# Scratch matrices of a chunked recurrence in DRAM: laid out by rows of all slots, diagonal blocks moved in four transfers

## The reference

```python
def rwkv7_scan(r, w, k, v, kk, a, reverse):      # 16 heads of 64, f32
    def step(state, inp):
        r_t, w_t, k_t, v_t, kk_t, a_t = inp
        sa = jnp.einsum('bhvk,bhk->bhv', state, kk_t)
        state = (state * w_t[:, :, None, :]
                 - sa[..., None] * (kk_t * a_t)[:, :, None, :]
                 + v_t[..., None] * k_t[:, :, None, :])
        return state, jnp.einsum('bhvk,bhk->bhv', state, r_t)
```

## Time and profile before

| | us |
|---|---|
| median of 3 runs (lowest to highest) | 1600.93 (1599.67 to 1605.68) |
| the profiled execution, own time | 1600.83 |
| its span | 1599.0 |
| TensorE busy | 1461.1 (91%) |
| VectorE busy | 510.5 (32%) |
| ScalarE busy | 240.1 (15%) |
| GpSimd busy | 184.5 (12%) |

### The profile page before, as it was taken

The page is one execution under the profiler, slowest core; times in us unless marked ns, Lnnn a source line. Parts: engine busy times, 40 slices in busy tenths (PEclk is TensorE's granted clock), DMA queues, the critical chain, the costliest instruction groups (busy, mean ns, idle before and its releaser), DMA issues.

```text
span 1599.0 us, 26196 instructions
## 1 busy us (share of the span) xinstructions
PE 1461.1 (91%) x11376; PEld 735.6 (46%) x11376; DVE 510.5 (32%) x712; ACT 240.1 (15%) x478; POOL 184.5 (12%) x349
## 2 busy tenths in 40 slices
PE   7999999989888895899989989989989989989987
PEld 5344455878877653434324324324324324324322
DVE  6666534667664564101101101101101101101103
ACT  3333321222212121100000000000000000000002
POOL 1323504434333210000000000000000000000000
PEclk9999999999998997899999999999999999999999
DMA  9245577766765645499999999999999999999994
GB/s 302 66 158 185 183 264 161 176 136 133 149 111 127 263 172 210 187 428 425 421 428 422 425 427 426 425 425 427 423 426 426 425 424 428 423 425 427 422 425 184
DMA packets 186070, 500.47 MB, mean 313 GB/s; under 512 B 125904, under 2 KB 135248, under 8 KB 153216
## 3 DMA queue, kind: packets, MB, share of 16 engines
q1 hardware_dynamic: 180192, 479.31, 78.2%
q0 software_dynamic: 5792, 19.88, 3.6%
HBM read 470.83 MB, written 28.33 MB: 312 GB/s over the span
## 4 chain that ended last, share of the span: by engine, by line
PE 32%; DMA 23%; DVE 2%; issue 1%; ACT 1%; DVEq 0%; SPq 0%
DMA ring<-in_exp_w_up 23%; PE pD L1543 14%; PE pG L1504 6%; PE pU L1524 6%; PE pX L1492 4%; PE pG L1524 3%; DVE res L1652 1%; DVE hid L1670 1%; PE pX L1531 1%; ACT hidT L1613 0%; DVE res L1688 0%; ACT xin L1596 0%; PE pX L1560 0%; ACT xin L1628 0%; ACT L1631 0%
## 5 line engine op out<-in xcount | busy, mean ns | idle before, releaser
L1670 DVE TENSOR_TENSOR hid<-silu,pU 128x512 f32<-128x512 f32 x32 | 20.6, 684 | 774.5 <-PE pU L1524 774.5
L1524 PE MATMUL pU<-ring,xin 128*64 128x512 f32 x768 | 173.8, 597 | 37.8 <-DMA ring<-in_exp_w_up 37.8
L1524 PE MATMUL pG<-ring,xin 128*64 128x512 f32 x768 | 171.3, 595 | 11.4 <-DMA ring<-in_exp_w_gate 10.7
L1543 PE MATMUL pD<-ring,hidT 128*64 128x512 f32 x768 | 167.9, 593 | 2.1 <-ACT hidT L1613 2.1
L1504 PE MATMUL pG<-yexp,scatter 128*128 128x512 f32 x256 | 124.4, 618 | 3.6 <-DVE res L1652 1.9
L1524 PEld LDWEIGHTS pU<-ring,xin 128*64 128x64 f32 x768 | 52.3, 137 | 157.8 <-issue 92.0
L1524 PEld LDWEIGHTS pG<-ring,xin 128*64 128x64 f32 x768 | 53.0, 137 | 116.9 <-issue 97.6
L1543 PEld LDWEIGHTS pD<-ring,hidT 128*64 128x64 f32 x768 | 55.4, 137 | 107.7 <-issue 107.0
L1652 DVE TENSOR_TENSOR res<-res,pG 128x512 f32<-128x512 f32 x128 | 87.0, 687 | 45.9 <-PE pG L1504 45.9
L1504 PEld LDWEIGHTS pG<-yexp,scatter 128*128 128x128 f32 x256 | 40.6, 188 | 87.2 <-DVE res L1652 62.9
L1492 PEld LDWEIGHTS pX<-pick,y 128*128 128x128 f32 x512 | 59.8, 196 | 5.4 <-issue 3.4
(11 more groups left out here) (234 smaller groups left out, 1737.0 us busy)
## 6 DMA issues: line engine op xcount, KB each, us to landing
ring<-in_exp_w_gate SPq DMA_DIRECT2D x48, 2048.0 KB, 34.6
ring<-in_exp_w_up SPq DMA_DIRECT2D x48, 2048.0 KB, 27.8
ring<-in_exp_w_down SPq DMA_DIRECT2D x48, 2048.0 KB, 28.8
lent_slot<-in_exp_w_up SPq DMA_DIRECT2D x16, 2048.0 KB, 20.5
lent_slot<-in_exp_w_gate SPq DMA_DIRECT2D x16, 2048.0 KB, 31.8
lent_slot<-in_exp_w_down SPq DMA_DIRECT2D x16, 2048.0 KB, 33.8
lent_slot<-in_rw_w_in SPq DMA_DIRECT2D x8, 1024.0 KB, 12.6
scratch_sw<-tok POOLq DMA_DIRECT2D x8, 512.0 KB, 3.9
```

Of the source, the lines that this page charges most:

```text
L1524: mm = pe.matmul(psum[f // 2][HEAD * s:HEAD * s + HEAD, :], xin[:, k, e, :], w[:, FF * r + HALF * f:FF * r + HALF * f + HALF], start=k == ...
L1543: mm = pe.matmul(pD[h][HEAD * s:HEAD * s + HEAD, :], hidT[:, j, c, HEAD * s:HEAD * s + HEAD], w[:, 4 * half + 2 * s + c % 2, HALF * h:HALF ...
L1670: dve.tensor_tensor(hid[:, j, :], silu[:, j, :], pU[j][:, :], ALU.mult).then_inc(hid_done, 1)
```

## The change

Both scratch arrays are laid out as (s, e, h, t): row s of all 32 matrices together, 2048 floats. So a row of `X` or `XT` on one partition is one run of 4 KB, and the two score transfers write runs that touch each other. A diagonal block at position k of a matrix now starts at row 16 k and column 16 k, and the 128 of them no longer form one regular pattern: blocks with the same k do. So `NB` is loaded in four transfers of 32 partitions (k = 0 to 3), and each of the two inverses is written in four. `NB` and `XB` hold block k of matrix (e, h) on partition 32 k + 16 e + h. The semaphores `blocks_in` and `base_out` count 64 instead of 16 for each.

```diff
-SQUARE = SLOTS * HEAD * (HEAD + 1)
+PARTS = HEAD // BASE
...
-            "blocks": [1, 2 * SQUARE], "inverses": [2, 2 * SQUARE],
+            "blocks": [1, P * D], "inverses": [2, P * D],
...
-                             tok[:, :, :].rearrange("p z d -> p (z d)")[:, 0:2 * SQUARE // P]).then_inc(zeroed, 16)
+                             tok[:, :, :].rearrange("p z d -> p (z d)")[:, 0:D]).then_inc(zeroed, 16)
...
-            return scr[name][a].rearrange("(e h w) -> e h w", e=2, h=SLOTS)[e][:, 0:HEAD * HEAD].rearrange("h (s t) -> s h t", t=HEAD)
-
-        def diagonal(name, a):
-
-            return scr[name][a].rearrange("(k w) -> k w", k=P)[:, 0:BASE * HEAD].rearrange("k (s t) -> k s t", t=HEAD)[:, :, 0:BASE]
+            return scr[name][a].rearrange("(s e h t) -> e s h t", s=HEAD, e=2, h=SLOTS)[e]
+
+        def diagonal(name, a, k):
+
+            on = slice(BASE * k, BASE * k + BASE)
+            return scr[name][a].rearrange("(s g t) -> g s t", s=HEAD, t=HEAD)[:, on, on]
+
+        def part(k):
+
+            return slice(2 * SLOTS * k, 2 * SLOTS * k + 2 * SLOTS)
...
-                    sp.wait_ge(blocks_in, 16 * n)
+                    sp.wait_ge(blocks_in, 16 * PARTS * n)
...
-                sp.dma_start(NB[:, :, :], diagonal("blocks", 0)).then_inc(blocks_in, 16)
+                for k in range(PARTS):
+                    sp.dma_start(NB[part(k), :, :], diagonal("blocks", 0, k)).then_inc(blocks_in, 16)
...
-                    sp.dma_start(diagonal("inverses", a), XB[:, a]).then_inc(base_out[a], 16)
+                    for k in range(PARTS):
+                        sp.dma_start(diagonal("inverses", a, k), XB[part(k), a]).then_inc(base_out[a], 16)
                 for a, dst in ((1, X), (0, XT[n % 2])):
-                    sp.wait_ge(base_out[a], 16 * (n + 1))
+                    sp.wait_ge(base_out[a], 16 * PARTS * (n + 1))
...
-                pool.wait_ge(blocks_in, 16 * (n + 1))
+                pool.wait_ge(blocks_in, 16 * PARTS * (n + 1))
                 if n:
                     for a in range(2):
-                        pool.wait_ge(base_out[a], 16 * n)
+                        pool.wait_ge(base_out[a], 16 * PARTS * n)
```

## The result

| | before | changed |
|---|---|---|
| median, us | 1602.26 | 1607.66 |
| runs, lowest to highest | 18, 1597.79 to 1612.31 | 18, 1602.91 to 1609.94 |
| profiled execution, span | 1599.0 | 1603.4 |

The ratio is 1.003 with a 95% interval of 1.0019 to 1.0041, which is 4.8 us slower (3.0 to 6.6). That lies within the 0.5% that the prediction called "no difference that shows", but it is a loss where a gain of 2.4 us had been forecast.

A forecast was written before the change was run, and what follows sets the result against it. TensorE and expert-weight loads end the chain; in the recurrence TensorE's turn and the DRAM trip are balanced. Trip terms -0.4 + 0.9 + 1.4 - 2.9 = -1.0 us a unit, keys +0.7, gave -2.4 us: 1598.5 us, range 1591 to 1608.

The forecast's parts named there:

- no difference that shows: The forecast's verdict on the whole kernel: the median stays within about 0.5%, 8 us, of before; chance 0.71.
- Scores out: Score transfers to DRAM (L640): issue less held up behind the XT return, -0.4 us a unit, bounds -1.0 and +0.5.
- NB in: Load of NB (L644): four quarters at 0.63 us an issue land later, +0.9 us a unit, bounds 0 and +1.7.
- Inverses out and XT's issue: L652, L660: eight quarters issued ahead of the return, 6.8 us against 5.4, +1.4 a unit, bounds -0.5 and +3.5.
- the slow rival: Quarters line up on SyncE's queue at 0.94 us each, trip +1.4 us a unit, keys +1.9: 1609 us; chance 0.20.
- XT in: Load of XT: with 4 KB runs 3.8 us against 6.7 from issue to fill, -2.9 a unit, bounds -0.7 and -3.0.
- The rival in which the parts cancel: Key loads take back the sooner return, or XT gains only 1 us: within 1.5 us of before, 1600.9; chance 0.15.
- trip: Round trip through DRAM, from scores going out to XT loaded and the fill starting: forecast -1.0 us a unit.
- Keys: Key loads (L625) behind NB on SyncE's queue: +0.7 us, bounds -0.4 and +1.9; turns 2 and 5 pay in full.
- walk: Turn-by-turn sum through the recurrence: unit 0 1.9 us earlier, unit 4 2.2, unit 7 2.4, so -2.4 us in all.
- The clock: TensorE's granted clock after waits: a wait shrunk to 1.3 us keeps it up, one grown to 2 loses it.
- Its own signs of being wrong: 4 KB returns over 5 us; an issue under 0.45 or over 0.8 us; fills of units 1 to 3 waiting.

## Why the prediction was wrong

- **What bounds the kernel**: right. Only the recurrence moved, and the rest followed one for one (4.8 us at its end, 4.4 in the span).
- **Scores out** (-0.4): -0.2. **NB in** (+0.9): +0.9. The price of an issue, 0.63, was 0.49 in the middle; but some were held, up to 1.37, so four took 2.4 us in the mean where 2.5 was counted. That the two cancel is luck.
- **Inverses out and XT's issue** (+1.4): +1.1. The bound from above (0.94 an issue) was not reached; the slow rival in its form, quarters that line up at 0.94, did not happen. A quarter lands 1.9 us after its issue, and the next goes out after 0.49, so they overlap; what adds up is the issue. The rule of the Trainium skill (DMA: Bandwidth & Descriptors, Rules for kernel authors) that transfers to disjoint halves of the partitions serialize is thus not what these quarters do. For the loads of `X` and `XT` its advice, one transfer of 128 partitions, agrees with the runs: 1.1 us sooner than two halves.
- **XT in** (-2.9): **the first step that failed.** It was -1.1. The price, 3.8 us, came from a lone transfer of 128 partitions, with the reason that "no other load is due". This one comes in two halves of 64 (1.1 us of the gap, by the kernel with one transfer) and while `X`, its own neighbour, is still coming (the rest; the traces bear it out, no kernel tried it). The rival in which the parts cancel had taken -1 here.
- The **trip** was thus +0.2 us, with GpSimd's stretch 0.5 shorter, and not -1.0. (The bounds of its parts add up to -4.5 and +5.0; "+3 or so" is a slip.)
- **Keys** (+0.7): **the second step that failed.** It was +1.3 by their landing, and the key waits rose by 6.3 us. The walk charged 1.6 us for them in all; one transfer for `NB` gave back 3.0. The forecast took the issues in their median only; unit by unit the keys landed 0.2 to 2.6 us later. That TensorE would pay for it in turns 2 and 5 was right (1.58 to 1.91, and 0.64 to 2.12 us); turn 4, counted as free, pays 1.66 as well. Behind the waits of turns 2 and 5 the clock fell too, some 1.6 us lost each time by the windows at the end, where it had stayed full before; nothing in the forecast stood for that.
- **The sum**: by the forecast's own walk, a trip of +0.2 and keys of +1.3 give about 3.5 us of loss (1.3 in turns 2 and 5, 0.8 in turn 3, 0.2 for unit 7). Measured 4.8. What the walk lacks is turn 4 and the clock behind the key waits; how much each carries was not separated. (Over the whole recurrence the low clock cost 8.5 us before and 10.2 after, by the traces' clock records.) The walk also sent most of the delay by the trip; in the changed kernel 3.0 of the 4.8 us went as soon as the keys no longer stood behind four transfers.
- **The clock**: forecast to stay up at unit 0 because the wait shrank. The wait grew to 2.74 us and the clock stayed up nevertheless (below): right for a reason that did not hold.
- **Chances**: no difference that shows had 0.71, and 1.003 is inside it; the side was wrong. The median of 1607.66 is close to the slow rival's 1609, but by luck: that rival had issues of 0.94 us and a trip of +1.4.
- **Its own signs of being wrong**: two of three came. The return with 4 KB runs takes over 5 us (5.72), and the fill of unit 1 waits (1.14).

## What to carry to other kernels

On a queue that issues everything, price a split transfer by what stands behind it: here the four quarters of `NB` cost some 3 us, and issues that only held up the keys behind `NB`, with `NB` landing as before, cost about as much. Take the price of a transfer from a row of the same shape (partitions, halves, company), not from one of the same run length. And before making a round trip faster, look whether its reader waits for all of it at once: moving one wait to its first reader gave more (5 to 9 us) than the long runs could without the quarters (2.7).

## What the runs showed of the hardware

A load of 4 KB runs into 64 partitions and then 64 more took 5.7 us for 512 KB, into 128 at once 4.6 us; the pitch in DRAM (4 or 8 KB) made no difference. In both, `X` is issued just ahead. An issue of 32 partitions for `NB` took 0.49 us in the middle, one of 128 with four times the runs 0.37 in the old layout and 0.56 in the kernel with one transfer out of the new one; the four of `NB` hold the queue for 1.91 to 2.82 us.

The granted clock did not follow the waits as the rows before suggested. Windows of the changed kernel (bounds, length, busy time by engine, clock, DMA share, GB/s; before: the earlier trace rows), and below them turns 2 and 5 of the kernel before:

```profile
270.11:276.10 5.99, 5.99 (x171) 5.73 (x172) 3.32 (x4) 1.48 (x8) 0.00 (x0) 1.00 0.50 90
462.54:466.50 3.96, 3.96 (x82) 3.84 (x82) 1.97 (x4) 0.00 (x0) 3.10 (x12) 0.59 0.02 4
515.44:521.40 5.96, 5.96 (x128) 5.96 (x129) 1.38 (x2) 0.00 (x0) 1.90 (x1) 0.51 0.63 232
357.50:361.50 4.00, 4.00 (x90) 3.81 (x88) 3.29 (x5) 0.59 (x1) 3.37 (x9) 0.58 0.67 247
```

```profile
355.10:361.50 6.40, 5.67 (x174) 5.30 (x176) 5.38 (x7) 0.59 (x1) 5.46 (x13) 1.00 0.54 188
456.20:466.50 10.30, 8.92 (x274) 8.27 (x270) 8.86 (x10) 0.95 (x3) 8.90 (x18) 1.00 0.12 19
```

After a wait of 2.74 us the clock was full, and TensorE did more in 6 us (171 matmuls against 130); in the kernel before, after 2.28 us, it was 0.71. After waits of 2.12 and 1.91 us (462.54 and 355.93) it was at the 1.2 GHz level for most of the window, and in the same turns before, after 0.64 and 1.58 us, it was full. In the kernel before, the clock also stands at 0.57 from 322 to 326 us, in a turn without a wait for a transfer. A window of 3.96 us at 0.59 has lost 1.6 us. So a clock that falls moves 1.6 us or more from one place to another, and in these two kernels the length of a wait alone does not say where: a prediction should not count it at a single wait.
